# Constant products ahead of TensorE's waits, gate rows spread in two pieces, and one gate multiplication moved on VectorE

## The chip, the cores and the metric

The kernel runs on one core of one Trainium2 chip. The time is that of one execution on the device, in microseconds (us), and lower is better. Times inside the profile are counted from the start of the span, which is the time from the first to the last instruction.

## What is computed

Two models of two layers each run one after the other over 256 rows of width 1024, batch 1, all in f32. The change touches the first model. Cut to what matters:

```python
def first_block(x, c, w_ada, b_ada, w_in, ..., w_router, router_bias, w_exp_gate, w_exp_up, w_exp_down, ln2_g, ln2_b):
    cond = jax.nn.silu(c)
    for l in range(DEPTH):                                   # 2 layers
        mod = cond @ w_ada[l] + b_ada[l]                     # one row of 6 x 1024
        sh1, sc1, g1, sh2, sc2, g2 = [m[:, None, :] for m in jnp.split(mod, 6, axis=-1)]
        h = _layer_norm(x) * (1.0 + sc1) + sh1
        mix = _mixer(h, ...)                                 # attention branches, merged @ w_o
        x = _layer_norm(DN_ALPHA * x + g1 * mix, ln1_g[l], ln1_b[l])
        h = _layer_norm(x) * (1.0 + sc2) + sh2
        ffn = _moe(h, w_router, router_bias, ...)            # 16 experts in 4 groups; a row's 2 are of one group
        x = _layer_norm(DN_ALPHA * x + g2 * ffn, ln2_g[l], ln2_b[l])
    return x

def _mixer(...):
    ...
    merged = g_a * (out_a @ w_pa) + g_b * (out_b @ w_pb)
    return merged @ w_o

# second_block(x, mem, ...): two layers of another model, which begins with rms_norm(x) and a product for mem
```

`g1` and `g2` are gates: one row of 1024 numbers that multiplies every row of a branch's result.

## The kernel before

Every engine has a program of its own, written out as a Python function that issues its instructions in order: `program_pe` (TensorE), `program_act` (ScalarE), `program_dve` (VectorE), `program_pool` (GpSimd) and `program_sp` (the DMA queue). Nothing is scheduled by a planner. An engine waits for named events of the others (`wait_ge(*at(...))`), which are raised by `then_inc(*up(...))`. The rows are two tiles of 128, t = 0 and 1.

**Weights.** They come as units of 1 MB into a ring of six buffers (`raw`). ScalarE rounds a unit to its high part (`whi`, L1409), VectorE subtracts it from the unit to get the low part (`low`, L2014), and a product of f32 values is three products of the rounded type: high by high, high by low and low by high (L585 to L587). `lo_made` is TensorE's wait for the low part. In VectorE's and ScalarE's programs `taken(unit)` stands where such a split is done.

**PSUM.** Eight banks go round in one queue. `bank(pe, key)` takes the bank at the head of the queue and waits for the events that free it; `leave(key, *events)` puts it back at the end and names these events:

```python
            b = turn.popleft()
            for event in free_at[b]:
                pe.wait_ge(*at(*event))
...
            free_at[where[key]] = events
            turn.append(where[key])
```

**A layer of the first model on TensorE.** `first_block` first lifts the normalised rows (`lift`, L603: transposes, then VectorE and ScalarE scale the columns, L2067 and L1452, and split them into high and low parts, L1459 and L2073). Then come the projections and attention. Four units `pa` (m = 0 to 3, 24 products each) follow. Each result is merged in a chain: VectorE multiplies (L2568), GpSimd adds (L2895), ScalarE rounds (L1796, `mg_hi`), VectorE subtracts (L2570, `mg_lo`). `out_proj` multiplies the merged rows by `w_o`; it takes four banks at once and then runs eight parts of 12 products of 512 columns. Between these places stand steps of the modulation (`mod_turn`, `mod_step` L718: four products 32 wide of 512 columns; `mod_sums` L737), whose weights come by DMAs of their own.

**The gate's row.** The columns of a gate stand in 128 partitions by 8 columns. `mod_row` turns them into eight rows (`crow`), and `mod_bcast` (L754) spreads each of these over 128 partitions with a product that has 8 rows on its inner side: two banks of four products. ScalarE copies both banks out (`bcast`, L1480). For gate 2 the place it copies to is still read by the merge, so there it waits first:

```python
                    if part == 2:
                        act.wait_ge(*at("mg_lo", "A", l, 3))
```

In the layers of the first model gate 2 is spread behind the four `pa` units; gate 5 is spread in the expert phase, after expert slot n = 17.

**Residual and router.** VectorE's `residual` has `half(t, c)` (gate times product, L2101; addition to x, L2104; statistics, L2105) and `whole(t)` (L2109 to L2117, which writes `x_new`). `moe` on TensorE transposes x (`xT`, L1013; the modulation's `x1` steps stand between the two tiles), multiplies it by the router's weights (`lt`, L1025), turns the logits (`rt`, L1031), counts places (`place`, L1042 and L1043) and gathers the sorted rows with a one-hot matrix (`gather`, L1054, 32 products of 256 columns). VectorE finds the groups, the one-hot matrix (ends with L2225), the ranks, and sorts and scales half of the gathered rows (L2303). Twenty expert slots follow, each with 24 + 12 products, and `put_back` (L1127) returns the rows to their places.

**The seams.** After layer 0, `residual_and_lift` on VectorE runs the last residual and the next layer's lift together: `half(0, 0)`, `half(0, 1)`, `whole(0)`, `half(1, 0)`, `lift` of tile 0, then `half(1, 1)`, `whole(1)`. After layer 1 the second model begins with its memory's projection (`mkv`); its two lifts, of `sid` ("B", 0, 1), stand between halves of these and the next projections, each behind 12 or 24 products.

## Time and profile before

| | |
|---|---|
| median of 3 runs | 1745.12 us (1743.94 to 1749.65) |
| the profiled execution | 1743.22 us |
| its span | 1741.4 us |
| mean granted clock of TensorE | 0.981 |
| instructions | 24621 |
| TensorE busy | 1671.8 us, 96% |
| VectorE busy | 1210.3 us, 70% |
| ScalarE busy | 932.9 us, 54% |
| GpSimd busy | 241.0 us, 14% |
| HBM read | 390.46 MB |

In the profile PE is TensorE's products, PEld its weight loads, DVE is VectorE, ACT is ScalarE, POOL is GpSimd and SP the DMA queue. A line L754 is a line of the kernel before. An f32 product is recorded as two instructions, so four products show as x8. The time in brackets is the engine's idle time just ahead of the group, with what ended it. The granted clock is a share of TensorE's full 2.4 GHz; it shows two levels, 1.00 and 0.50. An end of a product in a timeline is the end of its last result, about 0.17 us behind the time at which the next product can begin.

### The profile page before, as it was taken

What the parts mean: (1) busy time and instruction counts of PE and PEld (TensorE: products, weight loads), DVE (VectorE), ACT (ScalarE), POOL (GpSimd) and SP (SyncE); (2) the same over time, 40 slices, a digit from 0 to 9 for tenths busy, and PEclk for the clock granted to TensorE, in tenths of its full rate; (3) what the DMA queues carried; (4) which work ended last, traced back from release to release, by engine and by line L of the source; (5) the groups of instructions that cost most, each with busy time, mean ns of one, the idle gap of its engine ahead of it and who ended that gap; (6) DMA issues with size and microseconds to landing.
All of it is one profiled execution on the core that took longest, in us unless ns stands there. A gap on an engine that the chain in (4) does not pass through costs nothing.

```text
span 1741.4 us, 24621 instructions
## 1 busy us (share of the span) xinstructions
PE 1671.8 (96%) x10100; PEld 1413.2 (81%) x10100; DVE 1210.3 (70%) x1372; ACT 932.9 (54%) x1052; POOL 241.0 (14%) x216
## 2 busy tenths in 40 slices
PE   4999998999899998999989999999999999999999
PEld 2887876888689896788867899878888899978887
DVE  2547668899975857989986585566667655657664
ACT  4435545877544644688756463554436655445342
POOL 0420020000034001001016402000001710210000
PEclk8999998999999998999999999999999999999999
DMA  9975586999855245799938345556655634536552
GB/s 381 331 278 194 215 313 251 379 375 377 308 178 170 98 146 222 291 384 374 339 110 278 124 143 170 178 171 209 216 169 195 204 123 144 191 123 218 193 193 73
DMA packets 172479, 393.11 MB, mean 226 GB/s; under 512 B 6128, under 2 KB 110576, under 8 KB 150352
## 3 DMA queue, kind: packets, MB, share of 16 engines
q1 hardware_dynamic: 169952, 381.71, 61.9%
q0 software_dynamic: 1712, 7.50, 1.2%
q10 hardware_dynamic: 704, 2.33, 0.3%
q8 instruction: 81, 1.33, 0.3%
q14 instruction: 30, 0.25, 0.1%
HBM read 390.46 MB, written 1.05 MB: 225 GB/s over the span
## 4 chain that ended last, share of the span: by engine, by line
PE 76%; DVE 7%; POOL 6%; issue 5%; ACT 4%; DMA 1%; POOLq 0%; ACTq 0%; DVEq 0%
PE ps L585 18%; PE ps L587 18%; PE ps L586 18%; PE ps L645 6%; PE ps L646 3%; DVE low L2014 2%; PE ps L718 2%; ACT whi L1409 2%; POOL TB L2959 1%; PE ps L920 1%; PE ps L888 1%; PE ps L903 1%; PE ps L649 1%; DMA xs<-in_x 1%; PE ps L603 1%
## 5 line engine op out<-in xcount | busy, mean ns | idle before, releaser
L2014 DVE TENSOR_TENSOR low<-raw,whi 128x2048 fp32r<-128x2048 f32 x310 | 711.0, 2303 | 288.0 <-ACT whi L1409 286.3
L1409 ACT ACTIVATE whi<-raw 128x2048 fp32r<-128x2048 f32 x310 | 590.7, 1913 | 284.4 <-PE ps L587 215.9
L585 PE MATMUL ps<-HH,whi 128*128 128x256 f32 x960 | 275.6, 287 | 0.0
L586 PE MATMUL ps<-HH,whi 128*128 128x256 f32 x960 | 271.5, 283 | 0.0
L587 PE MATMUL ps<-HH,low 128*128 128x256 f32 x960 | 271.5, 283 | 0.0
L585 PE MATMUL ps<-whi,HH 128*128 128x512 f32 (+1 forms) x640 | 247.6, 387 | 17.4 <-DVE low L2014 7.2
L587 PE MATMUL ps<-whi,HH 128*128 128x512 f32 (+1 forms) x640 | 243.1, 380 | 0.0
L586 PE MATMUL ps<-low,HH 128*128 128x512 f32 (+1 forms) x640 | 243.1, 380 | 0.0
L585 PEld LDWEIGHTS ps<-HH,whi 128*128 128x128 f32 x960 | 183.9, 192 | 13.6 <-issue 13.2
L586 PEld LDWEIGHTS ps<-HH,whi 128*128 128x128 f32 x960 | 184.0, 192 | 0.0
L587 PEld LDWEIGHTS ps<-HH,low 128*128 128x128 f32 x960 | 183.9, 192 | 0.0
L645 PE MATMUL ps<-HH,whi 128*128 128x512 f32 x504 | 180.9, 398 | 0.0
L585 PEld LDWEIGHTS ps<-whi,HH 128*128 128x128 f32 x640 | 123.0, 192 | 50.1 <-issue 13.3
L587 PEld LDWEIGHTS ps<-whi,HH 128*128 128x128 f32 x640 | 122.9, 192 | 22.9
L646 PE MATMUL ps<-HH,low 128*128 128x256 f32 x504 | 141.4, 281 | 0.0
L586 PEld LDWEIGHTS ps<-low,HH 128*128 128x128 f32 x640 | 123.1, 192 | 20.8
L585 PE MATMUL ps<-whi,Bh 128*128 128x512 f32 x336 | 134.4, 400 | 1.6 <-DVE Bl L2144 1.6
L587 PE MATMUL ps<-whi,Bl 128*128 128x512 f32 x336 | 131.2, 390 | 0.0
L586 PE MATMUL ps<-low,Bh 128*128 128x512 f32 x336 | 131.1, 390 | 0.0
L645 PEld LDWEIGHTS ps<-HH,whi 128*128 128x128 f32 x504 | 94.8, 188 | 20.2
L646 PEld LDWEIGHTS ps<-HH,low 128*128 128x128 f32 x504 | 95.2, 189 | 3.0
L2822 POOL TENSOR_SCALAR small<-small 128x1 f32<-128x1 f32 (+2 forms) x30 | 26.9, 896 | 436.3 <-ACT AR L1808 183.6
(351 smaller groups left out, 2530.2 us busy)
## 6 DMA issues: line engine op xcount, KB each, us to landing
raw<-in_w_gu SPq DMA_DIRECT2D x80, 1024.0 KB, 5.2
raw<-in_w_ff SPq DMA_DIRECT2D x66, 1024.0 KB, 5.0
raw<-in_w_in SPq DMA_DIRECT2D x58, 1024.0 KB, 5.4
raw<-in_w_d SPq DMA_DIRECT2D x40, 1024.0 KB, 5.4
raw<-in_w_gate SPq DMA_DIRECT2D x32, 1024.0 KB, 5.4
ada<-in_w_ada_s SPq DMA_DIRECT2D x16, 1024.0 KB, 7.2
raw<-in_w_out SPq DMA_DIRECT2D x16, 1024.0 KB, 5.1
AR<-in_w_ada_s SPq DMA_DIRECT2D x13, 1024.0 KB, 8.8
```

The costliest lines, as they stand in the source:

```text
L585: pe.matmul(out, lhs[0], rhs[0], start=start, stop=False)
L586: pe.matmul(out, lhs[0], rhs[1], start=False, stop=False)
L587: return pe.matmul(out, lhs[1], rhs[0], start=False, stop=stop)
L603: ins = pe.transpose(b[:, j * P:(j + 1) * P], src[:, t, k * P:(k + 1) * P], ident)
L645: pe.matmul(b[:, :], hi, both, start=k == 0, stop=False)
L646: pe.matmul(b[:, S:2 * S], lo, H[0][:, k, :], start=False, stop=False)
L649: ins = pe.matmul(b[:, :], hi, both, start=False, stop=True)
L718: ins = pe.matmul(b[32 * g:32 * g + 32, :], cpad[:, k, :], mod_slot[s][:, 512 * g:512 * g + 512], start=a == 0, stop=last)
L888: ins = pe.matmul(b[:, qt * S:(qt + 1) * S], q[o:o + 64], k[o:o + 64], start=True, stop=True)
L1409: act.activation(wide(i, whi), wide(i, raw), ACT.Copy).then_inc(*up("w_hi", i))
L2014: dve.tensor_tensor(wide(i, low), wide(i, raw), wide(i, whi).bitcast(F32), ALU.subtract).then_inc(*up("w_lo", i))
L2822: step(pool.tensor_scalar(ap, ap, scale, eps, ALU.mult, ALU.add))
```

## The change

It adds `fill(b, n)`: n products of the identity with 256 constant columns into a bank that the next work overwrites. They stand behind the request for the bank and ahead of the wait for data, at these places: in `xT` ahead of tile 1 (3 in layer 0, 8 in layer 1), ahead of `lt`, `rt` and `place` (3 each), ahead of the gather (4), in layer 0 behind the modulation steps 38 and 39 in a bank of their own (6 each), and in the lifts at the seam to the second block (18 for tile 0, 9 for tile 1). `mod_bcast` now spreads one half at a time: for gate 2 behind `pa` 1 and `pa` 2, for gate 5 behind expert slots 17 and 18, where ScalarE's copies are split too. And `half` is cut into `gated` (the multiplication) and `added`; in `residual_and_lift` the `gated(1, 1)` now stands ahead of the lift of tile 0.

```diff
+LIFT_FILL = {("B", 0, 1, 0): 18, ("B", 0, 1, 1): 9}
@@ lift
                     b = bank(pe, "lift", sid, t, kq)
                     if kq == 0:
+                        fill(b, LIFT_FILL.get((*sid, t), 0))
                         pe.wait_ge(*at(*ready))
@@ mod_bcast
-            def mod_bcast(l, part):
-                for h in range(2):
-                    b = bank(pe, "bcast", l, part, h)
...
+            def mod_bcast(l, part, h):
+                b = bank(pe, "bcast", l, part, h)
+                if h == 0:
+                    pe.wait_ge(*at("crow", l, part))
+                for j in range(4):
+                    kk = 4 * h + j
+                    ins = pe.matmul(b[:, j * P:(j + 1) * P], ident[0:8, kk:kk + 1].broadcast_to([8, P]),
+                                    crow[0:8, 0:P], start=True, stop=True)
+                ins.then_inc(*up("mm", "bcast", l, part, h))
+                leave(("bcast", l, part, h), ("bcast", l, part, h))
+
+            def fill(b, n):
+                for _ in range(n):
+                    pe.matmul(b[:, 0:S], ident, cons[:, P:P + S], start=True, stop=True)
@@ first_block, behind each pa unit
                         leave(key, ("pa_in", l, m))
-                mod_bcast(l, 2)
+                        if m in (1, 2):
+                            mod_bcast(l, 2, m - 1)
                 mod_turn(l, "out")
                 out_proj("A", l, lambda kk: ("mg_lo", "A", l, kk // 2))
@@ moe
                         b = bank(pe, "xT", l, t, kq)
+                        if kq == 0 and t:
+                            fill(b, (3, 8)[l])
...
                 lt = bank(pe, "lt", l)
+                fill(lt, 3)
...
                 rt = bank(pe, "rt", l)
+                fill(rt, 3)
...
                 b = bank(pe, "place", l)
+                fill(b, 3)
...
                 bs = [bank(pe, "gather", l, kp) for kp in range(4)]
+                fill(bs[0], 4)
...
-                    if n == 17:
-                        mod_bcast(l, 5)
+                    if n in (17, 18):
+                        mod_bcast(l, 5, n - 17)
...
                     for s in MOD_TAKEN[0]["ff"]:
                         mod_step(s)
+                        if s in (38, 39):
+                            b = bank(pe, "fill", s)
+                            fill(b, 6)
+                            leave(("fill", s))
@@ ScalarE
-                    if n == 17:
-                        bcast(l, 5, T1[:, 1024:2048])
+                    if n in (17, 18):
+                        bcast(l, 5, T1[:, 1024:2048], n - 17)
@@ VectorE, residual_and_lift
-                half, whole = residual(*what)
+                half, whole, gated, added = residual(*what)
...
                 half(1, 0)
+                gated(1, 1)
                 lift(sid, scale, bias, 0, *ready)
                 mod_turn(1, "in")
-                half(1, 1)
+                added(1, 1)
```

TensorE's order at the end of layer 0's `pa` units and the start of `out_proj`, before. `crow` is the eight rows of the gate, HH the merged rows, Bh and Bl the attention's results.

```order
L587 MATMUL ps<-Bh,low_53 128x256
L754 MATMUL ps<-crow,cons_s 128x128 [waits c_crow,c_pb_in]
L754 MATMUL ps<-crow,cons_s 128x128 x3
L754 MATMUL ps<-crow,cons_s 128x128 [waits c_wsum]
...
L718 MATMUL ps<-AR,cpad 32x512 [waits c_mod5]
L718 MATMUL ps<-AR,cpad 32x512 x3
L585 MATMUL ps<-whi,HH 128x512 [waits c_pa_in,c_w_lo,c_mg_lo,c_crow]
```

The same engine and place in the changed kernel, whose lines stand three or four further down (L588 to L590 for L585 to L587, L757 for L754, L722 for L718); lines of only "..." leave out products of the `pa` units.

```order
L590 MATMUL ps<-Bh,low_52 128x256
L757 MATMUL ps<-crow,cons_s 128x128 [waits c_crow,c_pb_in]
L757 MATMUL ps<-crow,cons_s 128x128 x3
L588 MATMUL ps<-Bh,whi 128x256 [waits c_w_lo,c_pb_in]
...
L757 MATMUL ps<-crow,cons_s 128x128 [waits c_pb_in]
L588 MATMUL ps<-Bh,whi 128x256 [waits c_w_lo,c_wsum]
...
L722 MATMUL ps<-AR,cpad 32x512 [waits c_mod5]
L588 MATMUL ps<-whi,HH 128x512 [waits c_bcast,c_w_lo,c_pa_in,c_mg_lo,c_crow]
```

The two groups of the spreading moved ahead of the third and the fourth `pa` unit, and the first product of `out_proj` has one more wait, `c_bcast`: its fourth bank is the one that the first half of the spreading left. In layer 1 the four banks of `out_proj` are freed by `wsum`, `crow` and `pa_in` in both kernels.

VectorE's order at the seam from layer 0 to layer 1, before. G holds the gated sums and, later, the lifted columns.

```order
L2105 BN_STATS small<-xs 128x6 [waits c_d_step]
L2067 TENSOR_SCALAR G<-ps,modT 128x128 [waits c_mod_cols,c_mm,c_d_step]
L2067 TENSOR_SCALAR G<-ps,modT 128x128 x3
L2073 TENSOR_TENSOR HH<-G,HH 128x4x128 [waits c_H_hi] x2
L2030 TENSOR_TENSOR modT<-ps,cols_s 128x4 [waits c_mm]
...
L2101 TENSOR_TENSOR G<-ps,T 128x512 [waits c_mm]
L2104 SCALAR_TENSOR_TENSOR xs<-xs,G 128x512 [waits c_res]
```

And in the changed kernel, where L2120 is L2101, L2086 is L2067, L2092 is L2073, L2049 is L2030 and L2125 is L2104:

```order
L2126 BN_STATS small<-xs 128x6 [waits c_d_step]
L2120 TENSOR_TENSOR G<-ps,T 128x512 [waits c_mm,c_d_step]
L2086 TENSOR_SCALAR G<-ps,modT 128x128 [waits c_mod_cols,c_mm]
L2086 TENSOR_SCALAR G<-ps,modT 128x128 x3
L2092 TENSOR_TENSOR HH<-G,HH 128x4x128 [waits c_H_hi] x2
L2049 TENSOR_TENSOR modT<-ps,cols_s 128x4 [waits c_mm]
...
L2125 SCALAR_TENSOR_TENSOR xs<-xs,G 128x512 [waits c_res]
```

The last multiplication of the residual went from behind the lift to ahead of it, and its addition stayed behind.

## Rows read from the trace of the kernel before

**Rows 1.** of the page: busy time of the engines, TensorE by slices, the chain by engine
```profile
PE 1671.8 (96%) x10100; PEld 1413.2 (81%) x10100; DVE 1210.3 (70%) x1372; ACT 932.9 (54%) x1052; POOL 241.0 (14%) x216
...
PE   4999998999899998999989999999999999999999
...
PE 76%; DVE 7%; POOL 6%; issue 5%; ACT 4%; DMA 1%; POOLq 0%; ACTq 0%; DVEq 0%
```

**Rows 2.** windows (busy us and count by engine, granted clock, DMA): the low stretches, and their sum
```profile
234.51:237.91 3.40, 3.40 (x9) 2.66 (x9) 1.29 (x2) 2.43 (x2) 1.34 (x2) 0.50 1.02 429
...
268.65:282.25 13.60, 12.40 (x57) 9.34 (x58) 9.47 (x42) 1.50 (x5) 0.00 (x0) 0.50 0.23 78
...
654.40:657.75 3.35, 3.35 (x9) 2.61 (x9) 1.89 (x2) 0.08 (x1) 1.27 (x1) 0.50 1.01 426
...
685.10:698.70 13.60, 10.44 (x55) 6.96 (x53) 11.31 (x39) 4.41 (x7) 0.55 (x1) 0.50 0.01 4
...
855.80:859.15 3.35, 3.35 (x9) 2.61 (x8) 3.35 (x5) 0.12 (x1) 0.00 (x0) 0.50 0.29 120
...
sum 64.10, PE 54.69 PEld 39.60 DVE 43.15 ACT 27.19 POOL 5.71; mean PE 5.47 PEld 3.96 DVE 4.31 ACT 2.72 POOL 0.57
```

**Rows 3.** timeline of PE (start, us, group [idle before]), layer 0, 217 to 235
```profile
217.63 0.70 PE L983 MATMUL ps<-AR,ones 128*128 128x256 f32 x2
...
231.35 2.05 PE L754 MATMUL ps<-crow,cons_s 8*128 8x128 f32 x16
...
234.32 0.66 PE L585 MATMUL ps<-whi,HH 128*128 128x512 f32 x1
```

**Rows 4.** timelines of DVE and ACT at the end of layer 0's merge
```profile
239.03 0.69 DVE L2570 TENSOR_TENSOR HH<-G,HH 128x512 fp32r<-128x512 f32 x1 [2.06 <-ACT HH L1796]
...
239.81 1.09 ACT L1480 ACTIVATE G<-ps 128x512 f32<-128x512 f32 x2 [0.82 <-DVE HH L2570]
```

**Rows 5.** timeline of PE in `out_proj` of layer 1
```profile
664.65 0.50 PE L585 MATMUL ps<-whi,HH 128*128 128x512 f32 x1 [0.39 <-DVE low L2014]
```

**Rows 6.** timeline of PE, router of layer 0
```profile
268.38 1.63 PE L737 MATMUL ps<-sel,AR 128*128 128x4 f32 x8
...
271.66 1.93 PE L718 MATMUL ps<-Bf,cpad 128*32 128x512 f32 x8
...
273.52 1.03 PE L1042 MATMUL ps<-TB,ones 128*128 128x12 f32 x4
...
276.17 6.75 PE L1054 MATMUL ps<-ARr 128*128 128x256 f32 x32 [1.20 <-DVE ARr L2225]
```

**Rows 7.** timeline of DVE, router of layer 0
```profile
266.56 2.29 DVE L2014 TENSOR_TENSOR low<-raw,whi 128x2048 fp32r<-128x2048 f32 x1
...
275.41 0.62 DVE L2225 TENSOR_SCALAR ARr<-AR,TB 128x256 fp32r<-128x256 f32 x2
...
280.82 1.00 DVE L2303 TENSOR_SCALAR T<-ps,modT 128x256 f32<-128x256 f32 x2 [0.43 <-PE ps L1054]
...
282.49 1.00 DVE L2303 TENSOR_SCALAR T<-ps,modT 128x256 f32<-128x256 f32 x2 [0.68 <-PE ps L1054]
```

**Rows 8.** timelines of PE and DVE, router of layer 1
```profile
684.37 1.30 PE L1013 MATMUL ps<-cons_s,xs 128*128 128x128 f32 x8 [2.24 <-DVE xs L2117]
...
699.33 0.99 DVE L2303 TENSOR_SCALAR T<-ps,modT 128x256 f32<-128x256 f32 x2 [0.60 <-PE ps L1054]
```

**Rows 9.** timeline of PE, seam from layer 0 to 1
```profile
473.72 1.94 PE L718 MATMUL ps<-ada,cpad 128*32 128x512 f32 x8 [2.27 <-DMA ada<-in_w_ada_s]
...
482.03 0.47 PE L585 MATMUL ps<-whi,HH 128*128 128x512 f32 x1 [2.83 <-DVE G L2101]
...
490.70 0.52 PE L603 MATMUL ps<-cons_s,T 128*128 128x128 f32 x3
```

**Rows 10.** timeline of PE, the two lifts at the seam to the second block
```profile
902.42 1.94 PE L603 MATMUL ps<-cons_s,T 128*128 128x128 f32 x8 [5.18 <-ACT T L1436]
...
919.41 1.07 PE L603 MATMUL ps<-cons_s,T 128*128 128x128 f32 x8 [2.58 <-ACT T L1436]
```

More of the change, by code:

```diff
@@ L745, in mod_row @@
                 leave(("row", l, part), ("crow", l, part))
-            def mod_bcast(l, part):
-                for h in range(2):
-                    b = bank(pe, "bcast", l, part, h)
-                    if h == 0:
-                        pe.wait_ge(*at("crow", l, part))
-                    for j in range(4):
-                        kk = 4 * h + j
-                        ins = pe.matmul(b[:, j * P:(j + 1) * P], ident[0:8, kk:kk + 1].broadcast_to([8, P]),
-                                        crow[0:8, 0:P], start=True, stop=True)
-                    ins.then_inc(*up("mm", "bcast", l, part, h))
-                    leave(("bcast", l, part, h), ("bcast", l, part, h))
+            def mod_bcast(l, part, h):
[11 more added lines that the diff above has]
+                    pe.matmul(b[:, 0:S], ident, cons[:, P:P + S], start=True, stop=True)
             def ffn(kind, l, n, sid, tail):
@@ L1473, in exps, with bcast @@
                 ins.then_inc(*up("exp", kind, l, i))
-            def bcast(l, part, out):
-                for h in range(2):
+            def bcast(l, part, out, *hs):
+                for h in hs or range(2):
                     act.wait_ge(*at("mm", "bcast", l, part, h))
@@ L2093, in residual, with gated @@
             def residual(l, which, part, y, gate, lng, lnb, tmp):
-                def half(t, c):
-                    v, sb, h = tmp[:, 1024 * t:1024 * t + 1024], small(4 + 12 * t, 12), slice(512 * c, 512 * c + 512)
+                def gated(t, c):
+                    v, h = tmp[:, 1024 * t:1024 * t + 1024], slice(512 * c, 512 * c + 512)
                     key, bank_of = y(t, c)
@@ L2100, in half, with added @@
                         dve.wait_ge(*at("bcast", l, part, c))
-                    ins = dve.tensor_tensor(v[:, h], ps(*bank_of)[:, :], gate[:, h], ALU.mult)
-                    ins.then_inc(*up("res", "A", l, which, t, c))
+                    dve.tensor_tensor(v[:, h], ps(*bank_of)[:, :], gate[:, h], ALU.mult).then_inc(*up("res", "A", l, which, t, c))
+                def added(t, c):
+                    v, sb, h = tmp[:, 1024 * t:1024 * t + 1024], small(4 + 12 * t, 12), slice(512 * c, 512 * c + 512)
                     dve.wait_ge(*at("res", "A", l, which, t, c))
@@ L2105, in half @@
                     step(dve.bn_stats(sb[:, 6 * c:6 * c + 6], x[:, t, h]))
+                def half(t, c):
+                    gated(t, c)
+                    added(t, c)
                 def whole(t):
@@ L2119, in whole @@
                     dve.wait_ge(*at("x_new", l, which, t))
-                return half, whole
+                return half, whole, gated, added
             def residual_and_lift(sid, scale, bias, ready, *what):
-                half, whole = residual(*what)
+                half, whole, gated, added = residual(*what)
                 half(0, 0)
@@ L2258, in moe @@
                 scale, bias, v = modc(l, 4), modc(l, 3), turned_rows(sid)
-                half, whole = residual(l, "out", 2, lambda t, c: (("out", "A", l, 2 * c + 1, t), ("out", "A", l, t, c)),
+                half, whole, *_ = residual(l, "out", 2, lambda t, c: (("out", "A", l, 2 * c + 1, t), ("out", "A", l, t, c)),
                                        G[:, 0:1024], G[:, 1024:2048], G[:, 2048:3072], T1)
@@ L2581, in first_block @@
                 else:
-                    half, whole = residual(*after)
+                    half, whole, *_ = residual(*after)
                     half(0, 0)
```

## The prediction

> **What bounds the kernel now.** I read these views, in this order. The page's table of engines and its chain: TensorE is busy for 96% of the span and is 76% of the chain that ended last, so a microsecond counts where TensorE waits or runs slowly, and elsewhere only if TensorE waits for it [rows 1]. The windows over the stretches at the lower clock level (0.50, which is 1.2 of 2.4 GHz): there are ten, 64.1 us in all [rows 2]; two are at the start, which the change doesn't touch, and eight can be touched. In the two routers (268.65 and 685.10) TensorE does short and narrow products between waits; the three at 234.51, 654.40 and 855.80 follow directly on the products that spread a gate's rows (L754). Then the timelines of TensorE, and beside them those of VectorE and ScalarE, for what waits there. In the expert phases the slices show TensorE at 9 throughout [rows 1], so time won ahead of them stays won.
>
> **The price of one constant product.** It is plain f32, 128 x 128 against 256 columns. The spreading did eight f32 products of 128 columns in 1.98 us (231.35 to 233.33), 0.248 us each; at twice the columns that bounds a fill to 0.50 us from above, and to 0.25 from below if the columns cost nothing. A product of exactly this shape took 0.70 us up to its last result (L983) [rows 3]. I take 0.44 us, nearest to columns doubling. So the fills take 1.3 us for 3, 1.8 for 4, 2.6 for 6, 3.5 for 8, 4.0 for 9 and 7.9 for 18, and twice as much at the lower level.
> The Trainium skill (TensorE: Matmul & The Clock Gate, Back-to-back issue gap) gives 262 cycles, 0.109 us, for 256 columns, whatever the type. By it the 18 fills would last 2.0 us. The spreading, with 0.248 us for half as many columns, does not agree with it.
>
> **Spreading in layer 0, gate 2: a new wait, +6.6 us.** The two halves move from behind the fourth `pa` unit to behind the second and third. Banks of PSUM go round in a queue, and `out_proj` asks for four at once before its first product. Before, its fourth bank was that of `pa` 2. Now it is the bank of the first spreading, and the order shows the new `c_bcast` in that row. That bank is free only when ScalarE has copied it (L1480), and this copy waits for `mg_lo` of part 3. The merge is a chain of VectorE, GpSimd and ScalarE that TensorE doesn't set: its fourth part ended at 239.72; the two copies ran from 239.81 to 240.90, the first of them until about 240.4 [rows 4]. TensorE began `out_proj` at 234.32 [rows 3] and will now begin at 240.4: +6.1 us. Nothing fills this wait. After so long an idle the clock will be low when the dense work comes back; the low stretches that dense work ended lasted 3.3 to 3.4 us [rows 2], which costs half, 1.7 us, as it did before here. If the rise comes later it may cost up to 3.4. I take 2.2, that is +0.5. Behind `out_proj` everything hangs on its last product, so nothing gives this back. Bounds +6.1 to +7.8.
>
> **Spreading in layer 1, gate 2: 0.** The order shows no new wait there. But TensorE waited at 664.65 for the low half of a weight that VectorE splits only after the merge [rows 5]. The 1.7 us of the low stretch before (half of 3.35 [rows 2]) go into that wait. Bounds 0 to -0.4.
>
> **Spreading of gate 5.** Layer 1: the low stretch of 3.35 us at 855.80 [rows 2] goes, and TensorE was dense: -1.7 us. Layer 0 had no such stretch in this execution: 0 here, up to -1.7 in another. Splitting at units 17 and 18 adds no wait that isn't long over.
>
> **Router of layer 0: -2.7 us.** Low from 268.65 to 282.25. At the full level the fills of the first three waits end 0 to 0.4 us behind their waits; the logits need VectorE, which splits a weight until 268.85 [rows 7], so that is hidden. The sums and the two modulation steps ran from 268.4 to 273.5, at the low level; at the full one they take some 2.7 us and end at 271.2, plus 1.3 of fills: `place` begins at 272.5 instead of 273.52, and its products, of which the first two took 1.03 us [rows 6], need half: the places come at about 273.3, some 1.7 earlier. `one_hot`, ready at 276.03 before [rows 7], is then ready at 274.3: -1.7. The gather of 32 products, 6.75 us almost wholly at the low level [rows 6], takes 3.4. From there VectorE sets the end: from `one_hot` to the end of the ranks it needs 4.36 us (276.03 to 280.39, where its wait of 0.43 began), so the first sorting starts at 278.65 instead of 280.82, and the second follows without its wait of 0.68: together -2.7 for the first expert's rows [rows 7]. The four fills ahead of the gather (until 274.9) cost 0.6 of TensorE's time and nothing of this chain. Bounds: -1.2, if only the gather's part comes, and -4.
>
> **Router of layer 1: -0.6 us.** The 8 fills need 3.5 us where the wait is 2.24, plus some 0.17 of draining: they put the last transposes off by 1.0 us. Behind them the logits are late by 0.8, since the low level no longer stretches their products; the groups too. `place` at the full level takes this back, so `one_hot` is ready as before, at 694.9. The sorting began at 699.33, after a wait of 0.60 for the gather, and this wait goes [rows 8]. Bounds -2 to +1.5.
>
> **Seam of the layers: -1.0 us.** The first weight product of layer 1 waited until 482.03 for a bank that the multiplication of the last expert sum (L2101) frees [rows 9]. It now stands ahead of the scaling, as the order shows, and the product is released by its own rows, at about 480.0. But the second row tile's lift came at 490.70 [rows 9], when its normalised rows were ready, and these depend on VectorE's chain, which is shorter by the 0.7 us multiplication and by some 0.3 from transposes at full level. So 2 us become 1.0. The 12 fills between the modulation steps put the last step off from 473.72 to some 474.5, but at the full level it takes 1.1 instead of 1.94 us and ends where it did [rows 9]. Bounds -0.5 to -2.
>
> **Seam to the second block: -0.2 us.** 18 fills last 7.9 us where TensorE waited 5.18; 9 last 4.0 where it waited 2.58 [rows 10]. The first lift begins about 2.4 us late, but at full level: its two halves are done 1.8 and 1.5 us late. The 12 wide products behind it run at the full level instead of mostly at the low one, and end as before. VectorE's chain for the second tile starts 1.5 late, and so comes its lift; the low stretch after it, 1.7 us of loss, goes. Bounds -2.5 to +3.
>
> **Sum:** 6.6 + 0 - 1.7 - 2.7 - 0.6 - 1.0 - 0.2 = +0.4 us. The profiled execution took 1743.22 us (span 1741.4), so 1743.6; the median of the runs shown is 1745.12, 1.9 above it, so 1745.5 on that footing. Since another execution may also lose gate 5's low stretch in layer 0, I forecast **1744.5 us**.
>
> **The rivals.**
> A, the spreading costs nothing: the bank's event is over in time, because the merge ends earlier than the old trace shows. For it: TensorE reaches `pa` 0 at the same time, and nothing new loads the merge. Against: L1480 never ran before `mg_lo`, and the merge's end is set by VectorE. Then +6.6 turns into -1.7: 1735.3 against the profiled execution, **1737** on the runs' footing, faster. Chance 0.13.
> B, the fills don't hold the clock in the routers, and run at the low level themselves at 0.88 us each. It decides if a low stretch still begins before 269 or 685 us in the old count. In router 0 the ten fills for logits, `place` and gather then take 8.8 us, against 2.2 of waits: +6.4, and in router 1 about +5, instead of -3.3: **1758**, slower. The low levels behind products with few rows speak for it; that fills use the full array speaks against. Chance 0.07.
> C, a fill costs what a product of the gather costs, of 256 columns too: 0.21 us at the low level (6.75 / 32 [rows 6]), 0.105 at the full one. The fills are then over long before the waits are, the routers and the last seam fall to the low level as before, and only gate 5 and the layers' seam gain: 6.6 - 1.7 - 1.0 = +3.9, **1748** on a footing between the two. The table of the Trainium skill named above (TensorE: Matmul & The Clock Gate, Back-to-back issue gap) is a rule for this case. Chance 0.05.
> D, the same mechanisms with the gains at their far bounds and the stall: -4 and -2.5 in the places that I put at -2.7 and -0.2, -2 in router 1: 1738 to 1741. Chance 0.10.
> The forecast's own case has 0.65 and spans 1740.5 to 1750.
>
> **How the numbers follow.** What a measurement of this kernel can tell from no change is about 0.3%, 5.2 us: 1739.9 to 1750.3. The forecast, C and a third of D lie within: 0.72. Faster: A, and most of D, 0.20. Slower: B and the upper end of the forecast's case, 0.08. The range is 1737 to 1750: it takes in A's value and the bounds of the forecast, and leaves out B.
>
> **What would show it.** In the changed profile: TensorE idle for about 6 us before the first product of `out_proj` in layer 0, released by L1480's copy (the line has moved by three), and a low stretch behind it; 1.00 as granted clock in both routers; the wait for L2101's bank gone from the layers' seam, and about 1 us left ahead of the second lift; the waits of 5.18 and 2.58 us gone, with both lifts some 1.5 to 2.5 us late against the products before them; no low stretch at gate 5. If `out_proj` starts without an idle, the forecast is wrong by 8 us; if a router shows 0.50, by some 6 in each.

## The result: 0.33% slower

The changed kernel took **1750.03 us** in the median (1748.05 to 1754.39), the kernel before 1744.06 us (1739.7 to 1749.65): a ratio of 1.0033, 95% interval 1.0025 to 1.0041. The forecast was 1744.5 us within 1737.0 to 1750.0, and "no change": the measured time lies just above the range, and the change made the kernel slower by more than can be put down to chance.

The page of the changed kernel, which answers to [rows 1] (busy time of the engines, TensorE by slices, the chain by engine):

```profile
PE 1690.3 (97%) x10252; PEld 1430.9 (82%) x10252; DVE 1210.3 (69%) x1372; ACT 932.7 (53%) x1052; POOL 240.8 (14%) x216
...
PE   5999989999999999999999999999999999999999
...
PE 77%; DVE 6%; POOL 6%; issue 5%; ACT 4%; DMA 1%; POOLq 0%; ACTq 0%; DVEq 0%
```

TensorE is busy for 18.5 us more than before, with 152 more records. The slices show what the change was about: the 8s at the routers and seams have become 9s, and one new 8 stands in slice 6, where `out_proj` of layer 0 begins. A busy TensorE has not made the kernel faster.

The windows over its low stretches, which answer to [rows 2] (two more of 6.8 us each are at the start, as before):

```profile
236.20:243.02 6.82, 3.44 (x8) 2.80 (x9) 2.89 (x2) 1.79 (x4) 2.57 (x4) 0.50 0.95 398
287.40:290.82 3.42, 3.42 (x9) 2.64 (x9) 2.88 (x4) 1.32 (x3) 0.99 (x2) 0.50 1.00 422
888.10:891.52 3.42, 3.42 (x10) 2.54 (x9) 2.73 (x8) 2.17 (x3) 0.00 (x0) 0.50 0.60 234
```

Of 64 us at the lower level 27 are left. Both routers and both seams now run at the full level. The three stretches stand in new places. The first is in and behind the new wait of layer 0. The second is in the first expert products behind router 0. It costs nothing: TensorE waited there 1.51 us for the low part of a weight before (at 288.74), and now doesn't wait. The third, at 888 us, is in the last expert work.

To see where the time went, both traces were laid side by side by what TensorE does. Each number is how much later (+) the kernel passes a place than the kernel before, less what it was late at 120 us (the start differs by about 1 us between executions). A column is a kernel, a row is the step from one place to the next, and the last row is the sum.

| stretch | after | e1 | e2 | e3 | e4 | e5 | e6 | e7 | e8 | e9 | e10 | e11 | e12 |
|---|---|---|---|---|---|---|---|---|---|---|---|---|---|
| to the end of `out_proj`, layer 0 | +6.5 | -0.9 | +6.5 | +7.1 | +6.9 | -1.6 | -1.1 | -1.1 | -1.2 | -0.9 | -1.7 | -1.6 | -1.1 |
| router 0 | -2.2 | -2.2 | 0.0 | -2.2 | -2.2 | -2.6 | -2.2 | -2.2 | -2.2 | -2.2 | -2.2 | -2.2 | -2.2 |
| experts, gate 5, layer 0 | +0.4 | +0.4 | 0.0 | +0.4 | +1.7 | 0.0 | 0.0 | +0.4 | +0.4 | 0.0 | +1.6 | 0.0 | 0.0 |
| seam of the layers | -1.0 | -1.0 | +2.3 | -1.0 | +0.2 | +0.5 | -1.0 | -1.0 | -1.0 | -1.0 | +2.3 | -0.5 | +0.4 |
| router 1 | -0.3 | -0.3 | +0.5 | -0.3 | +0.3 | -0.2 | -0.3 | -1.5 | -0.3 | -1.6 | -0.3 | -1.6 | -1.6 |
| gate 5, layer 1 | -1.2 | -1.2 | -1.6 | -1.2 | -1.2 | 0.0 | -1.6 | -1.2 | -1.2 | -1.6 | -1.6 | -1.6 | -1.6 |
| seam to the second block | +4.0 | +4.1 | +0.9 | -0.1 | -0.1 | -0.1 | +2.6 | -1.1 | 0.0 | -1.1 | +0.9 | -1.1 | -1.1 |
| sum | +6.2 | -1.0 | +8.6 | +2.7 | +5.6 | -4.0 | -3.7 | -7.7 | -5.5 | -8.3 | -0.7 | -8.5 | -7.1 |

(e1 to e12 are the experiments below; small steps between these places are left out, and are in the sum.) In the changed kernel two rows are positive and large.

**The wait of layer 0** is the first. Timelines of TensorE and ScalarE of the changed kernel (start, us, group, idle before it), beside [rows 3] and [rows 4]:

```profile
224.43 1.15 PE L757 MATMUL ps<-crow,cons_s 8*128 8x128 f32 x8
...
228.58 1.15 PE L757 MATMUL ps<-crow,cons_s 8*128 8x128 f32 x8
...
239.58 0.77 PE L588 MATMUL ps<-whi,HH 128*128 128x512 f32 x1 [5.79 <-ACT G L1499]
```
```profile
238.62 1.09 ACT L1499 ACTIVATE G<-ps 128x512 f32<-128x512 f32 x2 [0.82 <-DVE HH L2596]
```

The two rows of L757 are the two halves of the spreading. `out_proj` needs the bank of the first half, which TensorE finished at 225.6. It waits 5.79 us for the copy of that bank, the first of the two of L1499, and the copy waits for the merge.

**The seam to the second block** is the second. TensorE of the changed kernel, beside [rows 10]:

```profile
887.74 3.53 PE L1142 MATMUL ps<-Gr,ARr 128*128 128x512 f32 x8 [2.08 <-DVE Gr L2390]
...
899.48 7.93 PE L765 MATMUL ps<-cons_s 128*128 128x256 f32 x36
907.25 1.04 PE L607 MATMUL ps<-cons_s,T 128*128 128x128 f32 x8
```

and what the transposes could have had, and who waited for them, on ScalarE and VectorE:

```profile
902.04 1.15 ACT L1455 ACTIVATE T<-xs,small 128x1024 f32<-128x1024 f32 x1 [1.85 <-POOL small L2849]
```
```profile
907.96 1.13 DVE L2084 TENSOR_SCALAR AR<-ps,cols_s 128x128 f32<-128x128 f32 x4 [4.57 <-PE ps L607]
```

The 18 constant products are 36 records in 7.93 us, 0.44 us each. The normalised rows were there at 903.2, the products that turn them began at 907.25, and VectorE stood still for 4.57 us, where it had stood for 1.15 us before (at 903.62). The wait of 5.18 us before has become work of 7.93 us that nobody needs.

### The profile page after: what moved, and what is told of

It is laid out like the page before. It is cut to its first block, busy times and chain, and to the rows that moved or that the text cites. A ratio compares the mean times of both kernels' runs of the same rounds, so it can differ in the third digit from the quotient of the medians.

```text
span 1746.3 us, 24919 instructions
## 1 busy us (share of the span) xinstructions
PE 1690.3 (97%) x10252; PEld 1430.9 (82%) x10252; DVE 1210.3 (69%) x1372; ACT 932.7 (53%) x1052; POOL 240.8 (14%) x216
## 4 chain that ended last, share of the span: by engine, by line
PE 77%; DVE 6%; POOL 6%; issue 5%; ACT 4%; DMA 1%; POOLq 0%; ACTq 0%; DVEq 0%
PE ps L588 18%; PE ps L589 17%; PE ps L590 17%; PE ps L649 6%; PE ps L650 3%; PE ps L722 2%; DVE low L2033 2%; PE ps L765 2%; ACT whi L1428 2%; POOL TB L2985 1%; PE ps L928 1%; PE ps L896 1%; PE ps L911 1%; PE ps L653 1%; DMA xs<-in_x 1%
## 5 line engine op out<-in xcount | busy, mean ns | idle before, releaser
L588 PE MATMUL ps<-HH,whi 128*128 128x256 f32 x960 | 275.6, 287 | 0.0
L590 PE MATMUL ps<-HH,low 128*128 128x256 f32 x960 | 271.5, 283 | 0.0
L588 PE MATMUL ps<-whi,HH 128*128 128x512 f32 (+1 forms) x640 | 246.1, 385 | 24.0 <-DVE low L2033 6.4
L590 PE MATMUL ps<-whi,HH 128*128 128x512 f32 (+1 forms) x640 | 241.0, 377 | 0.0
L588 PEld LDWEIGHTS ps<-HH,whi 128*128 128x128 f32 x960 | 183.9, 192 | 13.6 <-issue 13.2
L590 PEld LDWEIGHTS ps<-HH,low 128*128 128x128 f32 x960 | 183.9, 192 | 0.0
L588 PEld LDWEIGHTS ps<-whi,HH 128*128 128x128 f32 x640 | 121.9, 190 | 57.2 <-issue 23.3
L590 PEld LDWEIGHTS ps<-whi,HH 128*128 128x128 f32 x640 | 121.9, 190 | 22.5
L588 PE MATMUL ps<-whi,Bh 128*128 128x512 f32 x336 | 134.4, 400 | 1.6 <-DVE Bl L2170 1.6
L590 PE MATMUL ps<-whi,Bl 128*128 128x512 f32 x336 | 131.2, 390 | 0.0
```

The source lines that it names most:

```text
L588: pe.matmul(out, lhs[0], rhs[0], start=start, stop=False)
L590: return pe.matmul(out, lhs[1], rhs[0], start=False, stop=stop)
```

## Experiments

Twelve kernels ran, each over five rounds beside the kernel before on the same chip. "Ratio" is to the kernel before, in brackets its 95% interval.

### e1: the bank of the wait alone

```diff
-                b = {(t, c): bank(pe, "out", kind, l, t, c) for t in range(2) for c in range(2)}
+                late = kind == "A"
+                b = {(t, c): bank(pe, "out", kind, l, t, c) for t in range(1 if late else 2) for c in range(2)}
...
+                if late:
+                    b.update({(1, c): bank(pe, "out", kind, l, 1, c) for c in range(2)})
```

The last two lines stand in `out_proj` between the products of the first row tile and those of the second.

> The changed kernel, but out_proj of block A asks for its two banks of the second row tile only after the products of the first, so its start no longer needs the bank of the first spreading. Theory (the stall of layer 0 is this bank and nothing else): out_proj of layer 0 starts without the idle of some 6 us, at about +0.6 us against the kernel before instead of +5.2 at its last product; the rest stands as in the changed kernel, so about 1743.5 us (6.5 less than its 1750.0). Rival (the merge or the split itself is late, whatever the bank): the idle stays, within 1 us of the changed kernel, 1749 to 1750. Second rival (the idle only shifts: the second row tile then waits for the bank instead): some 2 to 4 of the 6.5 us come back inside out_proj, 1746 to 1748.

Measured: 1742.11 us, ratio 0.9994 (0.9985 to 1.0003), 0.39% less than the changed kernel. `out_proj` begins without an idle, at the full level:

```profile
233.99 1.06 PE L725 MATMUL ps<-AR,cpad 128*32 128x512 f32 x8
234.98 0.50 PE L588 MATMUL ps<-whi,HH 128*128 128x512 f32 x1
```

The whole of the stall, 7.4 us in the table, is this bank. Both rivals fall: neither is the merge or the split late in itself, nor does the wait move into the second tile. The expected +0.6 us at the last product was -0.9, because the low stretch that the kernel before had here (234.51 [rows 2]) did not come.

### e2: the two pieces of gate 2 alone, on the kernel before

```diff
+                        if m in (1, 2):
+                            mod_bcast(l, 2, m - 1)
-                mod_bcast(l, 2)
```

> The kernel before, with one part of the change alone: the spreading of gate 2 in two pieces behind the second and third unit instead of after the fourth. Theory: the whole stall comes with it, +6.5 us in layer 0 at the first product after out_proj, nothing in layer 1, so about 1750.5 us (1744.1 before), and the later places of the changed kernel then gave it nothing in sum. Rival (the stall is part given back by the router's waits, since VectorE and ScalarE catch up meanwhile): +3 to +5 at the end, 1747 to 1749. Rival (splitting is free and the stall needs the other edits too): 1744.

Measured: 1752.04 us, ratio 1.0054 (1.0040 to 1.0069). The stall is there with the same wait:

```profile
239.82 0.77 PE L585 MATMUL ps<-whi,HH 128*128 128x512 f32 x1 [5.80 <-ACT G L1481]
```

The +6.5 us stand in the table, and the router gives nothing of them back (0.0), so that rival falls. But the kernel is slower than the stall makes it: at the seam of the layers it loses 2.3 us more. Two windows of e2 follow. The first is router 0, as low as before. The second is the seam, low for 13.66 us, where the kernel before had 3.4 us ([rows 9] shows one modulation step of it, 1.94 us):

```profile
274.10:287.76 13.66, 12.46 (x58) 9.40 (x58) 9.54 (x42) 1.53 (x5) 0.00 (x0) 0.50 0.24 78
478.90:492.56 13.66, 11.83 (x43) 7.48 (x44) 10.17 (x23) 3.78 (x7) 2.07 (x2) 0.50 0.36 131
```

### e3 and e4: no constant products in the lifts; none at all

```diff
-LIFT_FILL = {("B", 0, 1, 0): 18, ("B", 0, 1, 1): 9}
+LIFT_FILL = {}
```

In e4 `fill` does nothing at any of its places.

> The changed kernel without the 18 and 9 constant products in the lifts of the seam to the second block; these compute nothing that is used. Theory (the 18 are too many: they run some 4 us past the moment when the rows are ready): the first lift begins some 4 us earlier, at the lower clock level with its waits back, low stretches of 6 to 7 and some 3.4 us return there, and the sum is 1.5 to 2.5 us less than the changed kernel: about 1748. Rival (the fills are worth their time, because the low level costs as much): no difference or slower, 1750 to 1751. Rival (the late lift comes from the low stretch near 888 us and not from the fills): the lift stays late by over 3 us, 1750.

> The changed kernel with none of its constant products; these compute nothing that is used. Theory: the routers fall back to the lower clock level (loss 2.2 us in layer 0's, 0.3 in layer 1's, some 0.5 at the seam of the layers) and the lifts of the last seam win about 2 back, so 1750.0 to 1751.5, within 0.1% of the changed kernel. Rival (fills gain much in the routers and cost nothing at the seam): 1753 to 1755. Rival (fills cost everywhere more than they give): 1746 or less.

Measured: e3 1745.99 us, ratio 1.0013 (1.0003 to 1.0024), 0.20% below the changed kernel; e4 1748.67 us, ratio 1.0032 (1.0020 to 1.0044), no different from it. e3 is 4.0 us under the changed kernel, where 1.5 to 2.5 were expected, and e4 lies 1.3 us below the range of its theory. In e3 the first lift stands where its rows are ready, in slow products and behind a wait, and the last seam costs -0.1 us instead of +4.0:

```profile
904.96 1.94 PE L607 MATMUL ps<-cons_s,T 128*128 128x128 f32 x8 [3.75 <-ACT T L1455]
```

The 27 constant products of the lifts cost more than the slow level that they prevent. In e3 the low stretch near 889 us is still there and costs nothing, since the wait behind it is 3.75 instead of 5.18 us: it only hurts in the changed kernel because the products fill the wait. In e4 the lifts win the same 4.1 us, and 3.1 go elsewhere: 1.2 at the layers' seam, 0.6 in router 1, and 1.3 among layer 0's experts, where TensorE waits once for VectorE's low part of the activations:

```profile
312.13 0.47 PE L588 MATMUL ps<-whi,Bh 128*128 128x512 f32 x1 [1.10 <-DVE Bl L2368]
```

Router 0 lost nothing in this execution (-2.2), though it had no constant product: it was low for 6.8 us, not 13.6. Its theory expected the 2.2 us to be lost.

The granted clocks of all executions say the same of the whole kernel. Worked out from them (twice the missing share of the clock, times the span), TensorE was at the low level for 67 us of an execution of e4 on the average, and for 29 us of one of the changed kernel. The 76 constant products took 37 us off the low level, and the time is no better for it.

### e5: the earlier multiplication alone, on the kernel before

`gated` and `added` are defined as in the change.

```diff
                 half(1, 0)
+                gated(1, 1)
                 lift(sid, scale, bias, 0, *ready)
                 mod_turn(1, "in")
-                half(1, 1)
+                added(1, 1)
```

> The kernel before with one part of the change alone: the last expert sum multiplied ahead of the seam's scaling. Theory (the forecast's seam term without the part that came from fills): the first weight product of layer 1 no longer waits for VectorE's bank, the second lift comes 0.7 to 1.0 us earlier, nothing else moves: 1743.1 us, 0.4 to 1.0 below the kernel before. Rival (the seam runs at the lower clock level without the fills and gives the gain back, as the run without any constant product suggests, where the seam gained nothing): 0 to -0.3.

Measured: 1742.67 us, ratio 0.9995 (0.9983 to 1.0007). This settles nothing by its time. The profiled execution was the fastest of the twelve, 1737.98 us. Its trace tells more, above all in the part that is the same as before. Up to the seam TensorE runs the same program, and yet the low stretch at 234.5 us is missing, and router 0 has this one instead of 13.6 us [rows 2]:

```profile
266.88:270.28 3.40, 3.40 (x20) 1.10 (x12) 2.65 (x12) 0.56 (x1) 0.00 (x0) 0.50 0.32 77
468.26:478.50 10.24, 9.24 (x37) 5.55 (x38) 7.38 (x19) 3.78 (x7) 0.54 (x1) 0.50 0.46 162
```

So one execution gained 1.6 and 2.6 us at places where the code is unchanged. A good part of the low stretches of one trace is a draw, and not a property of the code. At the seam this one drew a long stretch and was 0.5 late.

The other executions bear this out. Of the 28 of the kernel before that ran beside e1, the four with the lowest mean granted clock (0.978) took 1746.0 to 1748.2 us, and the five with the highest (0.983 to 0.987) 1739.9 to 1741.4.

### e6: e1 with gate 5 in one piece

```diff
-                    if n in (17, 18):
-                        mod_bcast(l, 5, n - 17)
+                    if n == 17:
+                        mod_bcast(l, 5, 0)
+                        mod_bcast(l, 5, 1)
```

> The run e1 (changed kernel, late banks for the second row tile) with gate 5 spread in one piece again, in both layers; everything else stays. Theory (splitting gate 5 only moves the low stretch of layer 1 from the spreading to the last place, where the expert rows are put back, and it costs 0.4 us in layer 0): no low stretch near 882 us, put_back at 2.25 instead of 2.99 us, layer 0 0.4 better; in layer 1 a low stretch of 3.4 us may return at the spreading (+1.3 to +1.7): 1741.7 to 1743.5, within 0.1% of e1. Rival (the split is what the last forecast took it for, a gain of 1.7 in layer 1 and of nothing else): 1743.8 and a low stretch behind the spreading, none fewer elsewhere.

ScalarE's two copies are in one piece again as well. Measured: 1739.67 us, ratio 0.9982 (0.9971 to 0.9992), 0.12% under e1 (the intervals overlap), and 2.0 us below the range of its theory. No low stretch stands behind the spreading, though it is one piece, and none near 882 us. The products that put the rows back, e1 above and e6 below:

```profile
881.66 2.99 PE L1145 MATMUL ps<-Gr,ARr 128*128 128x512 f32 x8 [2.06 <-DVE Gr L2393]
```
```profile
880.06 2.26 PE L1145 MATMUL ps<-Gr,ARr 128*128 128x512 f32 x8 [2.06 <-DVE Gr L2394]
```

In the table the split costs 0.4 us in layer 0 and as much in layer 1 (-1.2 against -1.6). The last seam costs +2.6 with 18 and 9 constant products and no low stretch ahead of them, +4.1 in e1 with one.

### e7 and e8: the lifts' constant products cut to their waits; left out

```diff
-LIFT_FILL = {("B", 0, 1, 0): 18, ("B", 0, 1, 1): 9}
+LIFT_FILL = {("B", 0, 1, 0): 8, ("B", 0, 1, 1): 5}
...
-                            fill(b, (3, 8)[l])
+                            fill(b, (3, 5)[l])
```

Both are on e1; e8 has `LIFT_FILL = {}` and keeps the 8 ahead of the last transposes.

> The run e1 with constant products cut to the waits they stand in: 8 and 5 instead of 18 and 9 in the lifts to the second block, 5 instead of 8 ahead of the last transposes in layer 1's router. Theory (each constant product beyond the wait costs 0.44 us, each within it is free and holds the clock): the first lift at about -5 us against the kernel before instead of -1.15, its transposes in 1.04 us, no or one low stretch there; router 1 1.0 better at the transposes, little of it left: 1742.1 - 4.0 - 0.5 = 1737 to 1738. Rival (what matters is the low level that 18 suppress): the low stretches return with 8 and 5 and the gain is under 2, 1740 to 1741.

> The run e1 without constant products in the lifts to the second block; they compute nothing that is used. Theory: as in the run e3 against the changed kernel, 4 us less than e1: 1738.1, with low stretches of 6 to 7 us at the lifts; if e7 is right that the level can be held within the waits, this stays 0.5 to 1.5 above e7. Rival (their cost in the changed kernel came from the stall's shift of phase): within 1 us of e1, 1741 to 1743.

Measured: e7 **1735.19 us**, ratio 0.9952 (0.9935 to 0.9969); e8 1738.03 us, ratio 0.9974 (0.9963 to 0.9985). TensorE of e7 at the first lift:

```profile
890.42 3.61 PE L768 MATMUL ps<-cons_s 128*128 128x256 f32 x16
895.68 1.09 PE L607 MATMUL ps<-cons_s,T 128*128 128x128 f32 x8 [1.65 <-ACT T L1458]
```

The eight end 1.65 us ahead of the rows, the level holds, and the last seam gains 1.1 us, where 18 and 9 lose 4.1 and none gains nothing. e7 was better than expected by 2 us. Two sizes were off: the lifts won 5.2 us against e1 instead of 4.0, since the low stretch near 883 us went too, and router 1 won 1.3 instead of 0.5 with 5 products for 8 (three of 0.44 us each): nothing behind them hid it.

### e9 to e12: what is worth keeping

e9 is e7 with gate 5 in one piece (the edit of e6). e10 is the kernel before with the constant products of the two routers only (the change's `fill` calls in `moe`). e11 is e9 with gate 2 spread after the fourth unit, as before:

```diff
-                        if m in (1, 2):
-                            mod_bcast(l, 2, m - 1)
+                mod_bcast(l, 2, 0)
+                mod_bcast(l, 2, 1)
```

e12 is e9 without these lines:

```diff
-                        if s in (38, 39):
-                            b = bank(pe, "fill", s)
-                            fill(b, 6)
-                            leave(("fill", s))
```

> The run e7 (late banks; 8 and 5 constant products in the lifts, 5 in layer 1's transposes) with gate 5 spread in one piece again. Theory (splitting gate 5 costs 0.4 us in each layer and gives nothing, as e6 against e1 showed): 0.8 us less than e7, 1734.4, at most one low stretch behind the spreading (+1.6 if it comes). Rival (e6 was better than e1 only because its low stretch near 882 us went, which e7 had lost already, and the split does save the one at the spreading): 1735 to 1737.

> The kernel before with the constant products of the two routers alone (3, 3, 3, 3 and 4 in layer 0; 8, 3, 3, 3 and 4 in layer 1). Theory: -2.2 us in layer 0's router, -0.3 in layer 1's, as the changed kernel's trace showed: 1740.4 to 1741.5. Rival (the router's low stretches come and go between executions anyway, the run e5 had only 3.4 us of them in layer 0 without any constant product, so fills there gain on the average less): 1742 to 1743. Second rival (a low stretch kept out of the router comes back at the next weak place): the same time with the low stretch elsewhere, at the seam of the layers or the last experts.

> The run e9 with gate 2 spread after the fourth unit again, so that of the whole change only the constant products (cut to size) and the earlier gated sum are left. Theory (splitting gate 2 costs 0.64 us in each layer and saves the low stretch behind the spreading only where there is one, 1.6 us in layer 0): between -0.8 and +1.0 us against e9, 1733.6 to 1735.4. Rival (the split is what holds the level at out_proj): +2 to +3, 1737, with a low stretch at 234 and 654 us.

> The run e9 without the 6 and 6 constant products between the modulation steps at the seam of the layers. Theory (they hold the level through two waits for DMA and the transposes behind them; without them low stretches of 3.4 to 10 us stood there): a low stretch returns near 470 us and with it 0.5 to 1.5 us: 1735 to 1736. Rival (the waits set the end and 5.3 us of constant products only delay the steps): -0.5 to 0, 1734.

Measured: e9 **1733.85 us**, ratio 0.9946 (0.9933 to 0.9959); e10 1741.54 us, 0.9988 (0.9978 to 0.9999); e11 1735.06 us, 0.9954 (0.9942 to 0.9967); e12 1735.56 us, 0.9954 (0.9941 to 0.9967).

e9 is the fastest of all, 0.54% under the kernel before and 0.87% under the changed one. Its five executions lie within 2.2 us of each other (1733.45 to 1735.61), as do the twelve of e6, and the 17 of the kernel before in e9's rounds within 7.9: with the level held nearly everywhere little is left to draw. Against e7 the sum of the table is better by 0.6, where the theory had 0.8, though the intervals overlap; likewise e11 and e12 against e9. The traces say what the times can't: in e12 a stretch of 10.2 us at the low level returns at the seam (+0.4 instead of -1.0 there). e11 had none behind the spreading in layer 0 and one of 3.4 us in layer 1, in the second case under the wait of [rows 5]; splitting gate 2 is worth nothing that these runs can tell.

e10 gained 2.2 us in router 0 and lost 1.6 and 2.3 at two places where it has no constant products:

```profile
415.00:433.76 18.76, 18.76 (x93) 15.33 (x92) 17.43 (x13) 14.53 (x13) 0.00 (x0) 1.00 1.01 369
433.76:437.18 3.42, 3.42 (x9) 2.64 (x9) 3.42 (x4) 0.82 (x2) 0.00 (x0) 0.50 0.56 235
471.30:484.96 13.66, 10.20 (x39) 6.27 (x40) 9.74 (x24) 3.79 (x7) 1.80 (x2) 0.50 0.43 160
```

(The first of these rows is the stretch ahead of the second.) Over its 11 executions the gain was 0.12%, 2.1 us, between theory and first rival. Whether the two stretches came because the router had none, or by the draw, one trace can't say. The granted clocks say that most of what was won did not come back, so the second rival falls for the most part. By them an execution of e10 was low for 46 us on the average (11 of them), one of the kernel before for 68 us (17 of them). That is 22 us less, where the two routers had 27.2 us in the trace of before [rows 2]. Whether the other 5 us moved elsewhere or were never there on the average stays open. The 22 us were worth 2.1 us of time, since VectorE sets the end of much of a router [rows 7].

## Why the prediction was wrong

**The step that failed is the term "Seam to the second block: -0.2 us", bounds -2.5 to +3.** It was +4.0. The count was right: 18 products last 7.9 us (7.93), the first lift is 2.4 us late by them alone (in e6 its offset goes from -6.2 to -3.8), and the rows of the second tile are ready 1.5 us late there, since VectorE's chain starts that much later. What failed is what the term made of this. TensorE of the changed kernel, and ScalarE's second rows:

```profile
912.27 0.47 PE L588 MATMUL ps<-whi,HH 128*128 128x512 f32 x1 [1.23 <-DVE G L2120]
...
920.56 4.05 PE L765 MATMUL ps<-cons_s 128*128 128x256 f32 x18
924.44 1.04 PE L607 MATMUL ps<-cons_s,T 128*128 128x128 f32 x8
...
939.76 0.47 PE L588 MATMUL ps<-whi,HH 128*128 128x512 f32 x1 [0.60 <-DVE low L2033]
...
970.36 0.63 PE L1222 MATMUL ps<-cons_s,AR 128*128 128x128 f32 x4 [0.80 <-POOL AR L2956]
```
```profile
922.04 1.15 ACT L1455 ACTIVATE T<-xs,small 128x1024 f32<-128x1024 f32 x1 [1.85 <-POOL small L2849]
```

The forecast let the second lift be as late as VectorE's chain, 1.5 us. It was 2.6 us late in e6. The 12 wide products behind the first lift did end about as before, but the one behind them waits 1.23 us for a bank that VectorE's multiplication frees, a wait that the term did not have (0.01 us before). So all that follows is 1.5 us late as well, and the nine constant products add 1.1 to it (3.9 us, in a wait of 2.58 and the 0.17 ahead of it). In the rows above the normalised rows were ready at 923.2 and the lift began at 924.44. And "the low stretch after it, 1.7 us of loss, goes" was right of TensorE and worth nothing. TensorE won 1.6 us there and gave 1.5 back in two waits, 0.60 us for VectorE's low part (none before) and 0.80 for GpSimd (0.18 before): both engines were still as late as the lift had left them. So e6 ended at +2.6.

The rest, 1.5 us, came from the low stretch at 888.1, inside the last expert work, which put the start of the 18 products off; the forecast had no stretch there. Filling the whole wait had removed the slack (5.18 us) that hid such things; e3, e8 and e10, without products in the wait, and e11, with 8, had the stretch too, and their first lift was no later for it. It stood in five of the six kernels that spread gate 5 in two pieces (not in e7) and in two of the eight others (e10 and e11). That the split invites it is not shown. With it the two lifts were 3.9 and 4.1 us late against the products before them, where the forecast's sign was 1.5 to 2.5; in e6 they were 2.4 and 2.6.

**The price of one constant product, 0.44 us:** right at every place. Rival C, with 0.105, is out.

**Gate 2, layer 0, +6.6 us:** +6.5 in the changed kernel, wait, releaser and place as forecast, and e1 removes it with the bank. The low stretch behind it was forecast as well. Against e1 and e5, which have no low stretch here, the stall is 7.4 and 8.1 us (the second with the 0.6 us of the split itself), since the kernel before also lost 1.6 at this place in its profiled execution. This is why the change looked cheaper by the old trace than it is.

**Gate 2, layer 1, 0:** 0.0. **Gate 5, -1.7 in layer 1, 0 in layer 0:** -1.2 and +0.4. Two mistakes in one term. The spreading in two pieces takes 1.15 us each against 2.05 [rows 3], with a gap to the work around them; that cost 0.4 us per gate (0.6 at gate 2) and was not in the sum. And the low stretch went in six of the eight kernels whose gate 5 is in one piece as well (-1.6 in e2, e6, e9, e10, e11 and e12; only the kernel before and e5 had it), so nothing shows that the split removed it.

**Router 0, -2.7:** -2.2. The constant products of the first three waits were to hide behind VectorE; they ended 0.2 to 0.3 us behind each wait, and VectorE got the logits 0.8 us late (it waited 0.42 us for them). So `one_hot` was ready 0.9 us earlier, and not 1.7. And e4 and e5, with no constant product here, had -2.2 and -2.6 as well: the gain was right for this pair of traces, and part of it is a draw. **Router 1, -0.6:** -0.3; the 8 products put the transposes off by 1.3 us, and this stayed to the end, where the forecast let `place` take it back: with 5 it is -1.6. **Seam of the layers, -1.0:** -1.0, by the path forecast: the first weight product waits for its own rows, and 0.83 us are left ahead of the second lift.

```profile
483.70 0.47 PE L588 MATMUL ps<-whi,HH 128*128 128x512 f32 x1 [1.26 <-DVE HH L2092]
```

But before's trace had drawn a mild seam, 3.4 us at the low level; where nothing holds it the runs had 6.8 to 13.7 us there (e2, e4, e5, e10, e12).

**Rivals.** A (the spreading costs nothing) is refuted by e1 and e2, B (the level isn't held in the routers) by the windows above. D did not come.

With the last term at +4.0, gate 5 at -0.8 and router terms as measured the sum is +6.2 against the profiled execution, where the forecast had +0.4. Of the 5.8 us between them the last seam is 4.2, gate 5 is 0.9 and the routers are 0.8; gate 2 gives 0.1 back. By the medians the change costs 6.0.

## What to carry to other kernels

Work that only keeps an engine warm has to end before the wait that it stands in is over, with room for the draw of an execution: cut to their waits the same constant products gained 1.1 us at the seam where the long ones lost 2.6 to 4.1. Before moving an operation that takes a buffer from a rotating queue, list which later request gets that buffer and what frees it: here one early spreading handed `out_proj` a bank tied to the end of another engine's chain, for 6.5 us, and asking for two banks later, without moving any work, took it away. A microsecond won on one engine counts only if the engines it waits for next are not late: TensorE's 1.6 us behind the second lift went into its next two waits.

And a low-clock stretch in one trace should be priced as a chance: the same code had it in one execution and not in the next.

## What was not expected of the hardware

Low stretches come and go at places with the same instructions: router 0 of the kernel before had 13.6 us [rows 2], of e5, the same up to there, 3.4; after the spreading of gate 5 in layer 1 the kernel before and e5 had one, e2 and e10 none. Not every one is a draw: all eight kernels with constant products in the routers and gate 2 in two pieces had one of 3.4 us in the first expert products of layer 0 (287.40 above), e10 and e11, with gate 2 in one piece, had none. Dense work doesn't keep them out: in e10 TensorE was busy for 18.76 of 18.76 us at the full level up to 433.76, and the next 3.42 us, as busy, were at the low one.

A product of 128 x 128 against 256 columns of plain f32 costs 0.44 us at the full level, four times the 0.109 us that the Trainium skill (TensorE: Matmul & The Clock Gate, Back-to-back issue gap) gives for 256 columns. The factor is what the Trainium skill (FP8 and Floating Point Precision, TensorE Precision Notes) states for f32 that isn't reduced: four passes through the array. The prediction's "whatever the type" was its own reading: the table names no type. The traces agree with both pages when they are taken together: four times 0.109 is 0.436.
